# A token gather moved behind the up product in a mixture-of-experts kernel

## The reference

```python
probs = jax.nn.softmax((xt @ w_router).astype(f32), axis=-1)
sel = probs + router_bias.astype(f32)
...                                   # the best group of 4, in it the best 2 experts
combine = jnp.einsum('tk,tke->te', w, jax.nn.one_hot(idx, N_EXPERTS, dtype=f32))
for e in range(N_EXPERTS):
    h = jax.nn.silu(xt @ w_gate[e]) * (xt @ w_up[e])
    y = y + combine[:, e:e + 1] * (h @ w_down[e]).astype(f32)
```

## Time and profile before

| | |
|---|---|
| median of 3 runs | 782.25 us |
| the runs | 780.06, 782.25, 782.52 us |
| the profiled execution | 780.76 us |
| its span | 778.7 us |
| granted PE clock, mean over the span | 0.991 |
| PE busy | 740.8 us (95%) |
| PE's weight loads busy | 450.5 us (58%) |
| DVE, ACT, POOL busy | 335.4, 253.5, 29.0 us |
| moved by DMA | 251.41 MB, mean 323 GB/s |

### The profile page before, as it was taken

One profiled execution on the slowest core, in us unless ns is written; L12 is line 12 of the kernel. 1 busy time (PEld: TensorE's weight loads), 2 busy tenths in 40 slices (PEclk: granted clock), 3 DMA queues, 4 the chain that ended last, 5 costly groups with the idle time before them and its releaser, 6 DMA issues.

```text
span 778.7 us, 12250 instructions
## 1 busy us (share of the span) xinstructions
PE 740.8 (95%) x4334; PEld 450.5 (58%) x4335; DVE 335.4 (43%) x783; ACT 253.5 (33%) x537; POOL 29.0 (4%) x59
## 2 busy tenths in 40 slices
PE   6999999999999999999999999999999898898894
PEld 5978789998889999743333333333333332333341
DVE  6687566545768777574212221222212212202205
ACT  5675535546767555421111101111111101111111
POOL 3032000000001000000000000000000000000000
PEclk9999999999999999999999999999999999999998
DMA  9795313335040866999999999999999999999994
GB/s 278 310 348 216 144 74 138 137 157 217 2 187 30 324 274 239 390 367 385 425 426 425 425 425 431 428 423 429 429 423 431 428 423 431 429 421 433 426 421 167
DMA packets 38530, 251.41 MB, mean 323 GB/s; under 512 B 6129, under 2 KB 13394, under 8 KB 24162
## 3 DMA queue, kind: packets, MB, share of 16 engines
q1 hardware_dynamic: 38352, 250.94, 78.9%
q10 hardware_dynamic: 146, 0.04, 0.0%
HBM read 249.92 MB, written 1.05 MB: 322 GB/s over the span
## 4 chain that ended last, share of the span: by engine, by line
PE 72%; SPq 14%; DMA 6%; DVE 4%; issue 1%; ACT 1%; ACTq 0%; DVEq 0%
PE ps L2194 28%; PE ps L1798 8%; PE ps L1800 8%; PE ps L1799 8%; DMA gate_x<-in_w_gate_e_dram 6%; SPq L583 3%; PE ps L2144 3%; SPq L602 2%; SPq L572 2%; PE ps L1875 2%; PE ps L2151 2%; PE ps L2132 2%; SPq L586 2%; DVE xc L1204 1%; DVE wlo L1190 1%
## 5 line engine op out<-in xcount | busy, mean ns | idle before, releaser
L2194 PE MATMUL ps<-raw,xg 128*64 128x512 f32 x512 | 117.0, 607 | 9.0 <-DMA raw<-in_w_gate_e_dram 5.9
L1798 PE MATMUL ps<-hi_h,whi 128*128 128x272 f32 (+1 forms) x384 | 111.6, 291 | 0.4 <-DVE wlo L1121 0.3
L1800 PE MATMUL ps<-hi_h,wlo 128*128 128x272 f32 (+1 forms) x384 | 109.3, 285 | 0.0
L1799 PE MATMUL ps<-lo_h,whi 128*128 128x272 f32 (+1 forms) x384 | 109.0, 284 | 0.0
L1121 DVE TENSOR_TENSOR wlo<-raw,whi 128x512 fp32r<-128x512 f32 x128 | 82.6, 687 | 38.6 <-ACT whi L751 38.0
L2194 PEld LDWEIGHTS ps<-raw,xg 128*64 128x64 f32 x512 | 38.0, 140 | 85.2 <-issue 75.8
L751 ACT CAST whi<-raw 128x512 fp32r<-128x512 f32 (+1 forms) x128 | 74.1, 619 | 14.6 <-PE ps L1800 12.3
L1798 PEld LDWEIGHTS ps<-hi_h,whi 128*128 128x128 f32 x384 | 72.3, 188 | 4.3 <-issue 2.5
L1800 PEld LDWEIGHTS ps<-hi_h,wlo 128*128 128x128 f32 x384 | 72.4, 188 | 0.0
L1799 PEld LDWEIGHTS ps<-lo_h,whi 128*128 128x128 f32 x384 | 72.3, 188 | 0.0
L2194 PE MATMUL ps<-gate_x,xg 128*64 128x512 f32 x256 | 57.1, 594 | 7.7 <-DMA gate_x<-in_w_gate_e_dram 7.7
(11 more groups left out here) (367 smaller groups left out, 1152.6 us busy)
## 6 DMA issues: line engine op xcount, KB each, us to landing
raw<-in_w_up_e_dram SPq DMA_DIRECT2D x16, 2048.0 KB, 34.1
gate_x<-in_w_gate_e_dram SPq DMA_DIRECT2D x16, 2048.0 KB, 37.1
raw<-in_w_down_e_dram SPq DMA_DIRECT2D x16, 2048.0 KB, 34.3
raw<-in_w_gate_e_dram SPq DMA_DIRECT2D x15, 2048.0 KB, 36.4
raw<-in_w_in_dram SPq DMA_DIRECT2D x28, 1024.0 KB, 9.1
down_x<-in_w_down_e_dram SPq DMA_DIRECT2D x8, 2048.0 KB, 38.0
up_x_right<-in_w_up_e_dram SPq DMA_DIRECT2D x16, 1024.0 KB, 38.8
up_x_left<-in_w_up_e_dram SPq DMA_DIRECT2D x8, 2048.0 KB, 37.7
```

The source lines that it names most:

```text
L1798: mm(o, w1, hi[:, k, c0:c0 + n], start=(k == 0), stop=False)
L1799: mm(o, w1, lo[:, k, c0:c0 + n], start=False, stop=False)
L1800: last = mm(o, w2, hi[:, k, c0:c0 + n], start=False, stop=(k == KB - 1))
L2194: last = mm(ps[r0:r0 + SLOTS, bank_no, :], lhs[:, k % 4, k // 4, :], w[:, k % 2, 512 * c:512 * c + 512], start=(k == 0), stop=(k == KB - 1))
```

## The change

The gather and the wait ahead of it are put behind the up product. The two waits ahead of the up product stay ahead of it.

```diff
             product(0, xg, B_GATE, s.gate_used)
 
-            pe.wait_ge(s.pick_ready, u * 2 + 4)
-            gather()
-
             pe.wait_ge(s.wpt_ready, u * 2 + 1)
             pe.wait_ge(s.base_made, TT * 2)
             product(1, xg, B_UP, s.up_used)
+
+            pe.wait_ge(s.pick_ready, u * 2 + 4)
+            gather()
 
             pe.wait_ge(s.acc_base, TT * 2)
             scatter(u + 1)
```

## The result

| | before | after |
|---|---|---|
| median of 20 runs | 781.26 us | 783.96 us |
| lowest and highest | 779.92 to 782.70 us | 781.84 to 786.69 us |
| the profiled execution | 780.76 us | 784.79 us |
| its span | 778.7 us | 782.6 us |
| mean granted PE clock | 0.991 | 0.994 |

The ratio is 1.0033, with a 95% interval of 1.0027 to 1.0040: the changed kernel is 2.7 us slower, about the 0.3% that I had called indistinguishable (the interval reaches to both sides of it). The time lies in the stated range, 0.3 us from the forecast. That closeness flatters it: with more runs the median of before fell from 782.25 to 781.26, and on that the forecast's 1.44 us give 782.7. Of the 2.7 us the forecast has about half.

The account below looks back on a forecast made before the run. PE works through buffered experts until some 590 us, then waits for the weight stream. Steady 0, stream 0 and last unit 1.44 on the three-run median 782.25 give 783.7 us; range 781.0 to 786.0.

Parts of the forecast that it names:

- Steady units: Units from 380 to 590 us: PE work stays 25.02 us each, so the change in time is 0.
- The wait for hs: Transposes' weight loads waiting for DVE's hs: possible gain of 0.36 us a unit, taken as 0.
- The last unit: Last expert: up starts 0.28 us earlier, the gather's 1.72 us then comes in full; 1.44 us longer, bounds 0 and 1.72.
- The first unit: First expert: up still starts at 351.93, waiting for DVE's base; down and its releases come 1.72 us later.
- So 0 for the stream, with bounds of 0 and 1.72 us.: Weight stream at expert 2's down half: issued 1.72 us late, it still flows 1.9 us before the up half has landed.
- The paragraph on the rings: At 360 to 370 us, some DMA engines could finish the up half early and idle; up to 1.72 us longer.
- rival 2: PE's clock falls after a longer gap, in the first unit or the last: 1.7 us longer there, up to 785.4; chance 0.08.
- One of the signs of being wrong: End of the stream: prediction wrong if the last weights land over 1 us later or earlier with the same start.
- Rival 1: Expert 2's down half, 365 to 370 us: its late release starves the stream, at most 1.72 us, up to 785.4; chance 0.17.
- Rival 3: Stream start: first up not held by DVE's base, releases up to 1.72 us earlier; result 780.2 to 781.7; chance 0.10.
- Rival 4: Last unit: the down product waits for weights in both orders, so the gather costs nothing; 782.3; chance 0.10.
- The chances: Whole kernel, with 0.3% (2.35 us) as the bound: same 0.68, slower 0.26, faster 0.06.

Follow-up runs that it names:

- ends_front: The changed kernel with the gather back in front of the up product in the first and last expert only; 781.30 us, ratio 1.0000 to before.
- first_front: The changed kernel with the gather back in front of the up product in the first expert only; 783.05 us, ratio 1.0020 to before.
- last_front: The changed kernel with the gather back in front of the up product in the last expert only; 782.87 us, ratio 1.0019 to before.
- last_twice: The changed kernel with the last expert's gather carried out twice behind the up product; 785.88 us, ratio 1.0058 to before.
- late_down_1: The changed kernel with the first expert gathering both in front of and behind up, and the last in front; 781.03 us, ratio 1.0001 to before.
- warm: The changed kernel with six small matmuls into an unused bank in the first unit's gap ahead of up; 782.66 us, ratio 1.0016 to before.

## Why the prediction was right and wrong

*Steady units: right, within the 0.7 us that the interval leaves.* `ends_front` changes only these and is at 1.0000. (An expert's 12.58 MB are mostly transfers of 2 MB and not 12 of 1 MB, as I wrote; the 29.5 us stand.) The wait for hs gives nothing, as I had it: in after the transposes' weight load still stands 0.37 us idle (the row at 762.03), though DVE's hs had been finished by 759.97.

*The last unit: right, to the hundredth in the profile.* 1.44 us was the forecast and 1.44 is in the profile of after, by both of its parts: up starts 4.90 us after the second gate half instead of 5.17, and from up to the down product it takes 11.30 us instead of 9.59. By the times it is less sharp: `first_front`, which has this cost alone, is 1.6 us over before (0.9 to 2.3), and `last_front` is 1.1 us under after. In `last_twice` one more gather costs 1.9 us, for a forecast of 1.72. The up product started 0.14 us after its left half had landed.

*The first unit: the step that failed is "So 0 for the stream, with bounds of 0 and 1.72 us."* Its result held for the case that it described: a down release 1.72 us late costs at most 0.9 us, by `late_down_1`. Its working was too generous, since it counted the margin to the last engine's landing and not to the first one's, which makes it 1.1 us instead of 1.9; that the result held so well has some luck in it. The paragraph on the rings saw this possibility and left it out of the sum. (It took the 385 GB/s of 360 to 370 us for a sign of it. The share of DMA is 0.99 there, so the engines were slower and not idle.) But the case did not occur. Under rival 2 I had worked out the 2.45 us gap myself, called it close to the harmful length, and still left its consequence out of the sum, because the row at hand had 2.66 us (the other fall of before, at 710 us, came behind 2.76). Three of the profiled kernels have that gap with nothing in it, after, `last_front` and `last_twice`, and all three show the fall right behind it; no other shows one there. In `last_front`, the timeline of the up product and the window behind its start:

```profile
352.73 8.78 PE L2194 MATMUL ps<-raw,xg 128*64 128x512 f32 x32 [2.45 <-issue]
```

```profile
353.30:356.70 3.40, 3.40 (x12) 1.20 (x10) 1.71 (x3) 0.00 (x0) 0.00 (x0) 0.50 0.98 402
```

The fall adds 1.7 us to up, the up release comes 1.7 us late instead of on time and the down release 3.4 instead of 1.72, and the queue runs dry twice. That is the second rival leading into the first, in the place and by the mechanism named. It costs 1.3 us by the medians (2.7 less 1.44) and 1.85 in the profiled pair, where the bound was 1.72. One of the signs of being wrong that the prediction names came true with it: counted from the first gate product, the last weights land 1.85 us later than before (766.9 - 343.04 against 764.4 - 342.39).

*Rival 1 in its own form* (the late down release alone starves the stream, for up to 1.72 us) fell with `late_down_1`, but for a part of up to 0.9 us. *Rival 2 in the last unit* did not come: waits of 1.24 us left the clock at 1.00. The Trainium skill, "TensorE: Matmul & The Clock Gate", section "HAM oscillation — how this bites in real kernels", describes short groups of matmuls that run slow one after the other, each behind a wait of some 3 to 5 us. Those waits are longer than any here. After 590 us this trace has such groups behind waits of up to 1.33 us, all at full clock, and behind the 2.45 us gap it has the fall. So the trace agrees that the length of the wait makes the difference, and shows that a wait shorter than the page's example is enough. *Rival 3* was right that the start of the stream has about 1 us to give and wrong about what holds it: up waited for DVE's base to the tenth of a microsecond, and once that was moved the gain came. *Rival 4* fell with `last_twice`, and in after the down product of the last unit waited for no weights.

*The chances.* 0.68 for the same and 0.26 for slower gave too little to what came, a difference right at the bound of 2.35 us: two terms of 1.4 and 1.3 us stood in one sum, and I had counted only the first. The forecast of 783.7 came out so near because the median of three runs that it started from, 782.25, lay 1.0 us above that of twenty and stood in for most of the missing term. That is luck.

What stays open: whether the clock falls in the first unit in every execution of after. Three profiled kernels show it, one execution each, at a mean clock of 0.993 to 0.994; profiles without a fall have 0.994 to 0.996. The other executions of after have 0.992 to 0.996, so the two at 0.996 (782.54 and 783.48 us, both under the median) may have gone without; the means don't settle it. The wider scatter of after, 4.9 us against 2.8, would fit that, the restarts of the stream or the distance of its engines.

## What to carry to other kernels

Work that fits into a wait cost nothing here, and moving it out of the wait can charge it in two places: where it lands, as in the last unit here, and by the idle gap that it leaves, as in the first. Look at the first and the last turn of a loop by themselves, since the turns between may be covered by a saturated stream and these are not. And where a gap is nearly as long as one that the trace shows to have cost clock, price the fall in the sum.

## What the runs showed of the hardware

A wait of PE of 2.45 us was followed by 3.4 us at 1.2 GHz in each of the three profiles that have it, as were the waits of 2.66 and 2.76 us in before. Waits of 1.15 to 1.33 us left the clock at 2.4 GHz, fifteen of them in after from 600 us on; a sixteenth was 0.25 us long. No profile has a wait of PE between 1.4 and 2.4 us behind 340 us. The waits of PE there (total us, times, longest):

```profile
PE ps L2194 <- DMA raw<-in_w_up_e_dram: 6.3, 6, 1.2
PE ps L2194 <- DMA raw<-in_w_gate_e_dram: 5.2, 4, 1.3
PE ps L2194 <- DMA gate_x<-in_w_gate_e_dram: 3.8, 3, 1.3
PE ps L2194 <- DMA up_x_left<-in_w_up_e_dram: 3.7, 3, 1.2
```

Six small matmuls of 1.6 us in the first unit's gap, which left 0.91 us of it, were enough to prevent the fall in both profiles that have them.

The 16 engines of one stream of transfers are not in step. Late in the stream the first and the last land their parts of one transfer 3.2 us apart in before, 2.3 in `late_down_1` and 4.7 in `warm`. Some of them can so be out of work while the transfer as a whole has not landed.

A stream that has run dry does not come back at its pace at once: in after 38% and 58% of the 427 GB/s are made in microseconds behind a restart (164 in 359 to 360, 246 in 370 to 371) although the share of DMA is back at 0.8 and above. In 357 to 360 us the engines are idle for 1.0 us (shares of 0.35, 0.82 and 0.83), and 0.54 MB move where 427 GB/s would have moved 1.28, which is 1.7 us lost. A release that comes too late costs more there than the idle time of the engines.
